# The gated delta rule stage: chunks of 64 tokens with both directions in one tile, instead of chunks of 128

## What is computed

```python
# one direction, chunks of c tokens; g is the cumulated log gate within the chunk
decay = where(tri, exp(g_t - g_s), 0)
lower = where(strict, (k * beta) @ k.T * decay, 0)
u = solve(I + lower, v * beta)
w = solve(I + lower, k * beta * exp(g))
attn = where(tri, q @ k.T * decay, 0)
def step(state, inp):              # over the chunks
    v_new = u - w @ state
    o = (q * exp(g)) @ state + attn @ v_new
    state = exp(g_last) * state + (k * exp(g_last - g)).T @ v_new
    return state, o
```

## Time and profile before

| | us |
|---|---|
| median of 3 runs (5663.3 to 5677.66) | 5666.66 |
| the profiled execution, its own time | 5657.43 |
| its span | 5655.6 |
| mean granted TensorE clock over the span | 0.85 of full speed |

### The profile page before, as it was taken

One profiled execution on the slowest core, in us unless ns is written; L12 is line 12 of the kernel. 1 busy time (PEld: TensorE's weight loads), 2 busy tenths in 40 slices (PEclk: granted clock), 3 DMA queues, 4 the chain that ended last, 5 costly groups with the idle time before them and its releaser, 6 DMA issues. The chain is left out here.

```text
span 5655.6 us, 62014 instructions
## 1 busy us (share of the span) xinstructions
PE 4152.1 (73%) x22628; PEld 3278.1 (58%) x22628; DVE 2158.2 (38%) x2988; ACT 1378.2 (24%) x2379; POOL 967.4 (17%) x839
## 2 busy tenths in 40 slices
PE   6597975647899996398978776478888860646993
PEld 1597445646444446288966652268888860545662
DVE  1311435231688872401134415434344437330112
ACT  0111232101344441110112215134444432101211
POOL 0000000000344441000011002133232225102001
PEclk9798886877899998699989887788989985858996
DMA  6222012330000002413122122521011124158994
GB/s 205 87 92 71 7 54 83 117 114 23 14 4 2 4 1 82 152 60 116 67 85 68 39 84 61 150 77 43 31 34 41 34 80 167 56 195 300 328 307 167
DMA packets 332032, 523.47 MB, mean 93 GB/s; under 512 B 58069, under 2 KB 219557, under 8 KB 328565
## 3 DMA queue, kind: packets, MB, share of 16 engines
q1 hardware_dynamic: 317418, 479.23, 25.3%
q0 software_dynamic: 7568, 25.70, 1.2%
q10 hardware_dynamic: 6912, 16.78, 0.8%
HBM read 379.61 MB, written 141.93 MB: 92 GB/s over the span
## 5 line engine op out<-in xcount | busy, mean ns | idle before, releaser
L444 PE MATMUL in_ps_p<-in_wh,h 128*128 128x352 f32 (+1 forms) x1536 | 356.1, 318 | 26.8 <-DVE in_wl L458 26.8
L444 PE MATMUL out_ps_p<-out_wh,m 128*128 128x256 f32 (+1 forms) x1408 | 292.1, 306 | 60.6 <-DVE out_wl L458 60.6
L444 PE MATMUL rest__ps_p<-rest__wh,h 128*128 128x388 f32 x1024 | 266.4, 341 | 20.2 <-DVE rest__wl L458 20.2
L444 PEld LDWEIGHTS in_ps_p<-in_wh,h 128*128 128x128 f32 x1536 | 264.1, 190 | 27.4 <-issue 15.5
L444 PEld LDWEIGHTS out_ps_p<-out_wh,m 128*128 128x128 f32 x1408 | 232.1, 195 | 72.5 <-issue 43.7
L1876 PE MATMUL cg_ps_p<-h,cg_wh 128*128 128x512 f32 x768 | 249.4, 407 | 14.3 <-POOL cg_wl L1855 14.3
L3152 PE MATMUL ex_ps_g<-ex_wgu,ex_xt 128*128 128x256 f32 x1024 | 234.2, 388 | 27.0 <-DVE ex_xt L3203 13.6
L444 PE MATMUL in_ps_p<-in_wl,h 128*128 128x352 f32 (+1 forms) x768 | 242.4, 316 | 0.0
L1698 DVE TENSOR_REDUCE lq_nc<-lq_ps_f 128x1 f32<-128x512 f32 (+1 forms) x384 | 214.6, 584 | 54.4 <-PE lq_ps_f L1552 50.8
L1653 ACT ACTIVATE lq_p<-lq_ps_s 128x512 f32<-128x512 f32 x320 | 191.0, 598 | 177.5 <-PE lq_ps_s L1574 168.2
L3152 PEld LDWEIGHTS ex_ps_g<-ex_wgu,ex_xt 128*128 128x128 f32 x1024 | 195.5, 193 | 60.6 <-DVE ex_xt L3203 19.2
(11 more groups left out here) (560 smaller groups left out, 9314.0 us busy)
## 6 DMA issues: line engine op xcount, KB each, us to landing
ex_wgu<-in_moe_w_gate_dram SPq DMA_DIRECT2D x32, 1024.0 KB, 8.3
ex_wgu<-in_moe_w_up_dram SPq DMA_DIRECT2D x32, 1024.0 KB, 10.7
ex_wd<-in_moe_w_down_dram SPq DMA_DIRECT2D x32, 1024.0 KB, 10.4
ada_w<-in_w_ada_dram SPq DMA_DIRECT2D x12, 2048.0 KB
yb<-ex_y SPq DMA_DIRECT2D x32, 512.0 KB, 6.3
p<-in_o SPq DMA_DIRECT2D x8, 1760.0 KB, 7.2
rest__w<-in_w_in_dram SPq DMA_DIRECT2D x8, 1552.0 KB, 10.0
rest<-rest__o SPq DMA_DIRECT2D x8, 1552.0 KB, 6.7
```

The source lines that it names most:

```text
L444: mm = te.matmul(ps[n % NB][:, 0:cw], a, b, start=n_ == 0, stop=n_ == len(todo) - 1)
```

## The change

`gdn_loop` goes, `gdn_rounds` comes in its place. A round r (16 of them, `NR`) takes 64 tokens forward and 64 backward; since the one counts up and the other down, they lie on opposite partition halves (`hs`), and one tile of 128 partitions holds both. All eight heads are done in a round, as two groups g of four. TensorE multiplies each half by itself: a product of the program is over 64 rows and 64 stationary columns, top half by top half, bottom half by bottom half, into the same PSUM bank.

The rounds are written out, not looped. `follow` gives the order on every engine: scheme A (`step_a`, ten steps i) for round r + 1 and both groups, and after it, at six of the ten steps, a part of scheme B (`step_b`) for round r. Scheme A turns k and q, makes the scores, turns L and runs the levels of the inverse; now a level is a product for the next power and the running inverse together (`big`), and a second one for the power's transpose (`small`), so that nothing is turned in a level. Scheme B multiplies k and q by the state (`ks`), makes v_new from X and (beta v - beta exp(g) k S) (`vn`), then updates the state and makes the output (`as`).

The cumulated gates of all chunks, their exponentials and their sums are made once before the rounds, with products of triangles (`tri`, `both`, `sel`). Gates and betas as rows are turned, written to DRAM (`rows_d`) and read back in each round, copied to 64 partitions. A table of decays for a round is made on GpSimd (`tables`: add the mask, multiply beta by the strict mask, subtract the gate of the row, and multiply the exponential by beta; four operations of 128x512) and ScalarE (one exponential of 128x512, ahead of step 0). GpSimd also scales v by beta (1024 columns a round) and the old state by its decay (four operations of 512 columns a round). ScalarE copies the turned k and q (512 columns a group), the turned L and each `small` (256 columns), v_new, and scales q S by exp(g) (four times 128 columns a group). SyncE issues, for each r: the rows of r + 2, k, q, v of r + 2, and the stores of r. There is one more clearing of semaphores (`recycle`) ahead of the stage.

The diff, cut to the order, the loads, TensorE and VectorE:

```diff
--- before.py
+++ after.py
@@ -2458,300 +2458,445 @@
-def gdn_loop(nc, ident, qk, c2, gs, tri, out):
...
+def gdn_rounds(nc, ident, qk, c2, gs, keep, rows_d, out):
...
+    half = lambda d, r: (r if d == 0 else NR - 1 - r) % 2
+    chunk = lambda d, r: r if d == 0 else NR - 1 - r
+    hs = lambda d, r: slice(half(d, r) * C, (half(d, r) + 1) * C)
...
+        ROUND = [(r, i) for r in range(-1, NR) for i in range(10)]
+        B_AT = {0: ("ks", 0), 1: ("vn", 0), 2: ("as", 0), 4: ("ks", 1), 5: ("vn", 1), 6: ("as", 1)}
+        def follow(step_a, step_b):
+            for r, i in ROUND:
+                for g in X2:
+                    if r + 1 < NR:
+                        step_a(r + 1, g, i)
+                if r >= 0 and i in B_AT:
+                    what, g = B_AT[i]
+                    step_b(what, r, g)
...
+        def load(r):
+            b = r % 2
+            for t, src, off, sem, wait in ((k, qk, GDN_COLS, k_in, (s_s, 2 * r - 2)), (q, qk, 0, q_in, None), (v, c2, 2 * GDN_COLS, v_in, (vb_s, r - 1))):
+                if r >= 2:
+                    if wait:
+                        sp.wait_ge(*wait)
+                    else:
+                        for g in X2:
+                            sp.wait_ge(a_qt[g], r - 1)
+                for d in X2:
+                    c = chunk(d, r) * C
+                    sp.dma_start(t[b][hs(d, r), :], src[c:c + C, off:off + DH * P]).then_inc(sem[b], 16)
...
+        def step_a(r, g, i):
+            b = r % 2
+            K = kq[g][b]
+            bg, sm = big[g], small[g]
+            b4 = bg[:].rearrange("p (h j n) -> p h j n", h=HG, j=2)
+            s3 = sm[:, 0:HG * C].rearrange("p (h n) -> p h n", h=HG)
+            if i == 0:
+                te.wait_ge(k_in[b], 32 * (r // 2 + 1))
+                if r:
+                    te.wait_ge(d_x[g], 5 * r)
+                for h in range(HG):
+                    tr = te.transpose(bg[:, h * P:(h + 1) * P], k[b][:, (g * HG + h) * P:(g * HG + h + 1) * P], ident)
+                tr.then_inc(a_kt[g], 1)
+            elif i == 1:
+                te.wait_ge(q_in[b], 32 * (r // 2 + 1))
+                if r:
+                    te.wait_ge(e_p[g], 5 * r)
+                for h in range(HG):
+                    tr = te.transpose(sm[:, h * P:(h + 1) * P], q[b][:, (g * HG + h) * P:(g * HG + h + 1) * P], ident)
+                tr.then_inc(a_qt[g], 1)
+            elif i == 2:
+                te.wait_ge(e_kt[g], r + 1)
+                te.wait_ge(e_qt[g], r + 1)
+                for h in range(HG):
+                    for d in X2:
+                        o = b4[hs(d, r), h]
+                        mm = te.matmul(o, K[:, h, 0, hs(d, r)], K[:, h, :, hs(d, r)], start=True, stop=True)
+                mm.then_inc(a_kk[g], 1)
+            elif i == 3:
+                te.wait_ge(lt_ok[g], r + 1)
+                for h in range(HG):
+                    for d in X2:
+                        rows = hs(d, r)
+                        mm = te.matmul(s3[rows, h], px[g][0][rows, h, 0, :], ident[rows, rows], start=True, stop=True)
+                mm.then_inc(a_lt[g], 1)
+            else:
+                j = i - 3
+                old, P_ = px[g][(j - 1) % 2], pn[g][(j - 1) % 2]
+                if j == 1:
+                    te.wait_ge(e_l[g], r + 1)
+                    te.wait_ge(at_ok[g], r + 1)
+                else:
+                    te.wait_ge(e_p[g], 5 * r + j - 1)
+                    if j <= 5:
+                        te.wait_ge(d_pt[g], 4 * r + j - 1)
+                    if j == 2:
+                        te.wait_ge(x0_ok[g], r + 1)
+                    else:
+                        te.wait_ge(d_x[g], 5 * r + j - 2)
+                js = slice(0, 1) if j == 1 else slice(0, 2) if j <= 4 else slice(1, 2)
+                for h in range(HG):
+                    for rows in (slice(0, C), slice(C, P)):
+                        mm = te.matmul(b4[rows, h, js], P_[rows, h, :], old[rows, h, js, :], start=True, stop=True)
+                mm.then_inc(lev_b[g], 1)
+                if j <= 5:
+                    for h in range(HG):
+                        for rows in (slice(0, C), slice(C, P)):
+                            mm = te.matmul(s3[rows, h], old[rows, h, 0, :], P_[rows, h, :], start=True, stop=True)
+                    mm.then_inc(lev_s[g], 1)
+        def step_b(what, r, g):
+            m, b = 2 * r + g, r % 2
+            col = lambda h: slice(h * P, (h + 1) * P)
+            if what == "ks":
+                if m >= 2:
+                    te.wait_ge(up_s, m - 1)
+                if m:
+                    te.wait_ge(vc_s, m)
+                    te.wait_ge(o_s, m)
+                for n, o in enumerate((b_ks, b_qs)):
+                    for h in range(HG):
+                        for d in X2:
+                            mm = te.matmul(o[hs(d, r), col(h)], kq[g][b][:, h, n, hs(d, r)], S_[g][d][:, col(h)], start=True, stop=True)
+                mm.then_inc(ks_s, 1)
+            elif what == "vn":
+                te.wait_ge(r_s, m + 1)
+                te.wait_ge(d_x[g], 5 * (r + 1))
+                for h in range(HG):
+                    for d in X2:
+                        mm = te.matmul(b_ks[hs(d, r), col(h)], xt[g][b][hs(d, r), h, :], rr[hs(d, r), col(h)], start=True, stop=True)
+                mm.then_inc(vn_s, 1)
+            else:
+                te.wait_ge(vt_s, m + 1)
+                te.wait_ge(up_s, m)
+                for h in range(HG):
+                    for d in X2:
+                        mm = te.matmul(b_s[d][:, col(h)], k[b][hs(d, r), (g * HG + h) * P:(g * HG + h + 1) * P], vnt[hs(d, r), col(h)], start=True, stop=True)
+                mm.then_inc(s_s, 1)
+                te.wait_ge(tm_s, m + 1)
+                te.wait_ge(at_ok[g], r + 1)
+                for h in range(HG):
+                    for d in X2:
+                        mm = te.matmul(b_qs[hs(d, r), col(h)], at[g][b][hs(d, r), h, :], vn[hs(d, r), col(h)], start=True, stop=True)
+                mm.then_inc(at_s, 1)
...
+        def step_a(r, g, i):
+            b = r % 2
+            b4 = big[g][:].rearrange("p (h j n) -> p h j n", h=HG, j=2)
+            if i == 2:
+                ve.wait_ge(a_kk[g], r + 1)
+                ve.wait_ge(t1_s, r + 1)
+                ve.tensor_tensor(px[g][0][:, :, 0, :], b4[:, :, 0, :], heads(t1[b], g), ALU.mult).then_inc(lt_ok[g], 1)
+                if r >= 2:
+                    ve.wait_ge(at_s, 2 * (r - 2) + g + 1)
+                ve.tensor_tensor(at[g][b][:], b4[:, :, 1, :], heads(dd[b], g), ALU.mult).then_inc(at_ok[g], 1)
+                ve.wait_ge(lt_ok[g], r + 1)
+                ve.tensor_tensor(px[g][1][:, :, 1, :], id4[:], px[g][0][:, :, 0, :], ALU.subtract).then_inc(x0_ok[g], 1)
+            elif i >= 4:
+                j = i - 3
+                new, old = px[g][j % 2], px[g][(j - 1) % 2]
+                ve.wait_ge(lev_b[g], 6 * r + j)
+                if j <= 4:
+                    ve.tensor_copy(new[:, :, 0, :], b4[:, :, 0, :]).then_inc(d_pt[g], 1)
+                if j == 2:
+                    ve.wait_ge(x0_ok[g], r + 1)
+                if j >= 3:
+                    ve.wait_ge(d_x[g], 5 * r + j - 2)
+                if j == 6 and r >= 2:
+                    ve.wait_ge(vn_s, 2 * (r - 2) + g + 1)
+                if j >= 2:
+                    o = xt[g][b][:] if j == 6 else new[:, :, 1, :]
+                    ve.tensor_tensor(o, b4[:, :, 1, :], old[:, :, 1, :], ALU.add).then_inc(d_x[g], 1)
+        def step_b(what, r, g):
+            m, b = 2 * r + g, r % 2
+            if what == "ks":
+                ve.wait_ge(ks_s, m + 1)
+                ve.wait_ge(vb_s, r + 1)
+                if m:
+                    ve.wait_ge(vn_s, m)
+                for h in range(HG):
+                    c = slice(h * P, (h + 1) * P)
+                    hh = g * HG + h
+                    ins = ve.scalar_tensor_tensor(rr[:, c], b_ks[:, c], ns[:, r, hh:hh + 1], vb[b][:, hh * P:(hh + 1) * P], ALU.mult, ALU.add)
+                ins.then_inc(r_s, 1)
+            elif what == "vn":
+                ve.wait_ge(vc_s, m + 1)
+                if m:
+                    ve.wait_ge(s_s, m)
+                ve.tensor_tensor(h3(vnt[:]), h3(vn[:]), wide(tl[:, r, g * HG:(g + 1) * HG], P), ALU.mult).then_inc(vt_s, 1)
+            else:
+                ve.wait_ge(s_s, m + 1)
+                ve.wait_ge(ds_s, 2 * m + 2)
+                for d in X2:
+                    ins = ve.tensor_tensor(S_[g][d][:], ds_[d][:], b_s[d][:], ALU.add)
+                ins.then_inc(up_s, 1)
+                ve.wait_ge(at_s, m + 1)
+                if m >= 2:
+                    ve.wait_ge(o_out[m % 2], 32 * (m // 2))
+                ve.tensor_tensor(oo[m % 2][:], tmp[:], b_qs[:], ALU.add).then_inc(o_s, 1)
...
@@ -3379,7 +3524,9 @@
-        gdn_loop(nc, ident, qk, c2, gs, [upper, lower], gdn)
+        rows_d = [dram(f"rows{i}", (2 * P, GC)) for i in X2]
+        recycle(nc, 60)
```

(59 more changed lines are left out.)

398 lines of the change are left out of this document (181 added, 217 removed).

## The result

The changed kernel takes 5221.23 us (median of 4 runs, 5216.8 to 5225.08) against 5664.98 us beside it: a ratio of 0.9215, 95% interval 0.9195 to 0.9236. The forecast was 5227. The profiled execution took 5224.09 us, 433.3 less than the one before. Between the profiled executions the forecast (5218) was 6 us too low, between the medians (443.8 apart) 6 us too high.

What follows compares the result with a forecast made beforehand. The old stage was taken as bound by TensorE for two thirds of each pass, an exposed front for the rest. New stage: 36 + 15 x 29.0 + 20 + 2 + 4 = 497 us against 936, 439 less: 5227 us, range 5185 to 5325.

Steps and rivals of the forecast that it cites:

- The edited stage is worth what its own stretch is: Whole kernel: stages run one after the other, so only this stage's 936 us, 16.5% of the span, changes.
- A record's cost: TensorE in a round: halves overlap fully, so 0.0555 us a record of 128 columns and 0.0278 of 64.
- a change of shape: TensorE in a round: each change of the array's shape costs some 0.16 us, 11 changes 1.8 us.
- Hand-offs: Waits between engines in a round: mostly covered, short by 0.3 us at v_new, 0.2 at level 1, 0.2 at level 6.
- The seam between two rounds: End of a round into the next: level 6 waits 0.2 us for the last copy; no wait named for the transposes.
- The allowance of 0.7 us a round: TensorE in a round: 0.7 us added for bursts at a lower clock, taking 28.3 us to 29.0.
- Other engines: In a round: VectorE 17.9 us, ScalarE 11.3 and GpSimd 11.3, all beside 27.6 us of TensorE.
- SyncE's queue: Load of k waits for the update, some 21 us into a round, lands 2.6 us later, 4 us spare.
- The ends: Before the first full round 36 us (25 to 55); after the last, scheme B twice at 10 us and the store.
- Row tiles one by one: Rival, 7%: row tiles of one bank cannot overlap on TensorE, 16.9 us a round more, 5488 us.
- issue at 56 ns: Rival, 5%: TensorE's instructions come too slowly, 66 us a round, 5808 us; decides from 48 ns an instruction.
- Late k: Rival, 15%: hand-offs or late k decide the round, 4 us a round more, 5287 us.

Runs made afterwards that it cites:

- e10_one_half: Changed kernel with turned L, levels, v_new and output done twice on the top half, not on the bottom one: 5487.63 us, 45.23 us a round.
- e5_scaling_twice: Changed kernel with GpSimd scaling the old state twice: 5226.85 us, ratio 0.9234, 28.9 us a round.
- e7_loads_last: Changed kernel with the loads for two rounds ahead issued after the stores instead of before: 5254.11 us, ratio 0.9283, 31.34 us a round.
- e3_small_twice: Changed kernel with every `small` product of the levels done twice: 5319.46 us, ratio 0.9407.
- e11_small_twice_few_bytes: e3_small_twice with loads of k, q and v cut to an eighth of their columns from the third round on: 5294.97 us, 33.3 us a round.
- e1_halves_in_turn: Changed kernel with four heads of one half before the other's in products whose row halves write one bank: 5309.11 us, 34.1 us a round.
- e6_groups_in_turn: Changed kernel with scheme A of group 0 ended before that of group 1 begins: 5378.96 us, 37.64 us a round.
- e2_b_after_a: Changed kernel with all of scheme B of a round behind all of scheme A: 5451.24 us, 44.36 us a round.

## Why the prediction was right

**Where the time is.** "The edited stage is worth what its own stretch is": 434.0 us of stage against 433.3 of execution. The forecast had 439, with 2 us set aside for one more clearing of semaphores. The clearing shows nowhere: from the last store of the stage ahead to the first load lie 4.90 us in both kernels.

**A record's cost.** 0.0555 and 0.0278 were forecast, 0.055 and 0.029 came. The reading of the earlier trace rows held, and e10_one_half shows that, for the products on row halves in one bank, the overlap is what it rests on. Two terms were small misses: 288 records of 64 columns cost 8.4 us, not 8.0, and a change of shape 0.13, not 0.16, so 1.5 a round and not 1.8.

**Hand-offs.** `vn` behind `rr`: 0.3 forecast, 0.20 in the trace. The seam between two rounds was mis-sized in part. The timeline of the changed kernel there:

```profile
3892.15 1.33 PE L2700 MATMUL dr_ps_big<-dr_px,dr_pn 64*64 64x64 f32 x32
...
3893.42 1.31 PE L2659 MATMUL dr_ps_big<-ident,dr_k 128*128 128x128 f32 x8
3893.53 0.42 DVE L2869 TENSOR_TENSOR dr_xt<-dr_ps_big,dr_px 128x256 f32<-128x256 f32 x1 [0.28 <-PE dr_ps_big L2700]
3894.07 0.42 PEld L2659 LDWEIGHTS dr_ps_big<-ident,dr_k 128*128 128x128 f32 x4 [0.24 <-issue]
...
3894.66 1.09 PE L2720 MATMUL dr_ps_ks<-dr_S,dr_kq 128*64 128x128 f32 x16
```

Level 6 of both groups takes 1.27 us where 32 records need 0.93, and the transposes of k 1.24 where 8 need 0.87. A change of shape (0.13) is in each of the two. That leaves 0.2 for level 6, as forecast, and 0.24 for the transposes of group 1, where the forecast had nothing: by the code these wait until VectorE has read X of that group out of the same bank, and their loads go on at 3894.07, just behind VectorE's end at 3893.95.

**The clock.** The allowance of 0.7 us a round wasn't used: 1.00 in the rounds. 28.3 without it, 29.0 with it, 28.6 measured; 15 rounds came 6 us under the forecast, and the start 12 us over it. That these two errors partly cancel is luck, and with it that the sum is nearer than its terms.

**Other engines.** VectorE 17.9 forecast and 16.2 measured, ScalarE 11.3 and 10.7, GpSimd 11.3 and 10.5. e5_scaling_twice shows the cover.

**SyncE's queue.** Right in kind, wrong in size: k is issued at 22.0 of a round, near the 21 forecast, but lands 4.1 us later (up to 6.2), not 2.6 as the earlier trace rows had it. q and v follow it at once, which is the likely reason but was not tried by itself. Spare is 0.5 to 3.3 us, not 4. The trace before had a queue with less in it; the landing time should have been taken from a stage whose DMA share is as high (0.34 here, 0.14 in the earlier trace rows).

**The ends.** This term was mis-sized most: 36 forecast, 48.3 measured, inside the bounds of 25 and 55. Loads, constants and gates took 13.3 us in place of 7; the row tables and GpSimd 16.5 in place of 15; scheme A alone 18.5 in place of 14, at a clock of 0.85. The chain through DRAM and GpSimd in the timeline:

```profile
3714.52 1.76 SPq L2559 DMA_DIRECT2D rows<-dr_gt  x4
...
3721.40 1.10 SPq L2552 DMA_DIRECT2D dr_gr<-rows  x2
...
3724.94 1.26 POOL L2594 TENSOR_TENSOR dr_gr<-dr_gr,dr_neg 128x512 f32<-128x512 f32 x1 [18.98 <-DMA dr_gr<-rows]
...
3731.27 3.68 PE L2674 MATMUL dr_ps_big<-dr_kq 128*64 128x128 f32 x32 [12.89 <-ACT dr_kq L2775]
```

The two scheme B and the store at the end took 24.1 us, forecast 24.

**The rivals.** Row tiles one by one and issue at 56 ns are refuted (0.055 us a pair's record; 24 ns an instruction in the rounds). Late k did not decide, but e7_loads_last makes it do so with a shift of 3.1 us, so it was near. The supply of instructions was a real rival with the wrong condition: not a fixed rate of 48 ns, but stops that come at 22.1 ns an instruction and only with bulk loads under way (e3_small_twice, e11_small_twice_few_bytes). The changed kernel, at 24.2 ns, has 9% fewer instructions a us than that.

## What to carry to other kernels

Products over 64 rows should come in pairs, one on each half, next to each other in the program, with as few changes of shape between them as possible: here a pair costs what one product costs, and a change 0.13 us. Once TensorE is full for 99% of a loop, look at what the DMA queue owes: a load's slack counts from issue to landing under the loop's own traffic, and a load that waits for nothing belongs ahead of one that waits. Written-out loops have more instructions to bring by DMA (152 packets in place of 80 here). Where TensorE's idle time is put down to "issue" behind a burst of loads, and moves through the list of instructions from round to round, shrink the loads in a test run and see whether it goes.

## What the runs showed of the hardware that was not expected

TensorE starts a product of a free half before earlier ones that queue for the other half (`small` at 3876.38, `big` at 3876.48 in e1_halves_in_turn), so one order of halves for another cost 5.4 us a round and not the 16.5 of real serial work (e10_one_half). Cutting the loads of k, q and v to an eighth removed stops of up to 2.5 us from an engine that reads none of them at that moment (e3_small_twice against e11_small_twice_few_bytes). And with 20% of its time idle in pieces of at most 1.3 us, TensorE kept a granted clock of 1.00 (e6_groups_in_turn); at 23% in pieces of up to 4.2 us it had 0.86 (e2_b_after_a), with falls behind waits of 1.2 and 1.4 us too.
